# First layer of a two-part transformer: input projections, recurrence and softmax attention in another order

## What is computed

```python
for l in range(DEPTH):                       # 2
    h = rms_norm(x, norm_mix[l]);  z = h @ w_in[l]        # 2560 columns: 20 tiles of 128
    (q_a, k_a, v_a, q_h, i_h, f_fw, f_bw, g_h, a_c, g_c) = jnp.split(z, splits, axis=-1)
    # norm and rotary embedding of q_a (4 tiles) and k_a (1 tile), then softmax attention
    o_att = block_attention(q_a, k_a, v_a)
    # gated recurrence, forwards and backwards, 4 heads of 64
    o_hg = hgrn2_bidirectional(q_h, i_h, f_fw, f_bw, g_h, lb_fwd[l], lb_bwd[l], hgrn_norm[l])
    # depthwise convolution of 31 taps over a_c * sigmoid(g_c), then layer norm and silu
    o_cv = conformer_conv(a_c, g_c, conv_w[l], conv_b[l], conv_ln_g[l], conv_ln_b[l])
    x = x + jnp.concatenate([o_att, o_hg, o_cv], axis=-1) @ w_out[l]
    h = rms_norm(x, norm_mlp[l])
    x = x + jnp.square(jax.nn.relu(h @ w_mlp_in[l])) @ w_mlp_out[l]
```

## Time and profile before

| | us |
|---|---|
| median of 3 runs (4218.06 to 4220.09) | 4219.88 |
| the profiled execution | 4220.85 |
| its span, to which all times below belong | 4218.7 |
| busy in the span: PE, DVE, ACT, POOL | 3820.5, 2100.5, 1303.2, 1276.6 |

### The profile page before, as it was taken

How to read it: one execution, slowest core, us unless ns; L and a number is a source line. 1 busy time by engine, 2 the same in 40 slices (tenths; PEclk the granted TensorE clock), 3 DMA queues, 4 the chain that set the end, 5 groups by cost and what they waited for, 6 DMA issues and landing times. The chain is left out here.

```text
span 4218.7 us, 46489 instructions
## 1 busy us (share of the span) xinstructions
PE 3820.5 (91%) x17918; PEld 2952.7 (70%) x17918; DVE 2100.5 (50%) x3346; ACT 1303.2 (31%) x2109; POOL 1276.6 (30%) x522
## 2 busy tenths in 40 slices
PE   6977999897889997899999989997999999989997
PEld 4656888664768885757777667885757777668886
DVE  3786644448865543352255355553362336346444
ACT  3432211243231112254423432112153432332112
POOL 2210444322024442213232234442213232324442
PEclk8966999999589998999999999998999999999998
DMA  2100233211013232202121123233212121212322
GB/s 97 45 26 2 94 95 95 76 50 50 1 46 97 96 94 103 67 31 75 56 70 60 61 63 93 94 95 108 76 31 75 53 73 50 70 56 92 95 94 69
DMA packets 80149, 292.61 MB, mean 69 GB/s; under 512 B 9617, under 2 KB 10929, under 8 KB 79409
## 3 DMA queue, kind: packets, MB, share of 16 engines
q1 hardware_dynamic: 77136, 278.49, 20.9%
q10 hardware_dynamic: 2784, 11.03, 0.8%
HBM read 285.30 MB, written 2.10 MB: 68 GB/s over the span
## 5 line engine op out<-in xcount | busy, mean ns | idle before, releaser
L205 POOL TENSOR_TENSOR w_lo<-w_raw,w_hi 128x1024 fp32r<-128x1024 f32 x518 | 1276.3, 2464 | 2895.5 <-ACT w_hi L191 2895.4
L191 ACT ACTIVATE w_hi<-w_raw 128x1024 fp32r<-128x1024 f32 x518 | 550.1, 1062 | 1818.4 <-PE acc L242 1759.2
L240 PE MATMUL acc<-hH,w_hi 128*128 128x512 f32 x1840 | 780.5, 424 | 174.2 <-DVE hL L303 91.4
L242 PE MATMUL acc<-hL,w_hi 128*128 128x512 f32 x1840 | 732.1, 398 | 0.0
L241 PE MATMUL acc<-hH,w_lo 128*128 128x512 f32 x1840 | 731.8, 398 | 0.0
L240 PEld LDWEIGHTS acc<-hH,w_hi 128*128 128x128 f32 x1840 | 356.0, 193 | 277.9 <-issue 145.6
L273 DVE TENSOR_TENSOR xT<-acc,xT 128x512 f32<-128x512 f32 x160 | 110.7, 692 | 638.8 <-PE acc L242 638.8
L241 PEld LDWEIGHTS acc<-hH,w_lo 128*128 128x128 f32 x1840 | 356.5, 194 | 79.3 <-issue 13.7
L240 PE MATMUL acc<-H,w_hi 128*128 128x512 f32 x1024 | 404.9, 395 | 5.8 <-issue 4.2
L242 PEld LDWEIGHTS acc<-hL,w_hi 128*128 128x128 f32 x1840 | 354.2, 193 | 78.9
L240 PE MATMUL acc<-midH,w_hi 128*128 128x512 f32 x1024 | 403.9, 394 | 4.2 <-issue 4.2
(11 more groups left out here) (329 smaller groups left out, 4734.8 us busy)
## 6 DMA issues: line engine op xcount, KB each, us to landing
w_raw<-in_stream SPq DMA_DIRECT2D x518, 512.0 KB, 3.5
cw<-in_cmpw ACTq DMA_DIRECT2D x2, 2048.0 KB, 9.0
mixed<-in_cmpw ACTq DMA_DIRECT2D x2, 2048.0 KB, 13.7
x_tok<-in_x SPq DMA_DIRECT2D x1, 2048.0 KB, 8.9
out<-f_tok SPq DMA_DIRECT2D x4, 512.0 KB, 2.6
stack<-Z ACTq DMA_DIRECT2D x8, 128.0 KB, 3.5
stack<-Z ACTq DMA_DIRECT2D x8, 127.8 KB, 3.5
masks_f<-in_masks SPq DMA_DIRECT2D x1, 960.0 KB, 10.8
```

Source lines behind the costliest of these rows:

```text
L191: act.activation(w_hi[:, u % WB, 0:w], w_raw[:, u % 2, 0:w], ACT.Copy).then_inc(hi_split, 1)
L205: pool.tensor_tensor(w_lo[:, u % WB, 0:w], w_raw[:, u % 2, 0:w], w_hi[:, u % WB, 0:w], ALU.subtract)\
L240: pe.matmul(acc[n % 2][:, :], wh, H[:, k, :], start=(k == 0), stop=False)
L242: last = pe.matmul(acc[n % 2][:, :], wh, Lo[:, k, :], start=False, stop=(k == nk - 1))
```

## The change

- **Order.** The units are streamed as: convolution (4), forget gates (4), recurrence q and v (4), then softmax q, k, v (6) and the recurrence's output gate (2). Stage `first_in` has the first 12 products with nothing else on PE; stage `hgrn` comes next with the last 8 (`late_in`) in its steps: run 0 takes 48 parts in 14 steps, run 1 takes 16 parts in 16 steps (`pace`). Norm and rotation of the softmax tiles are in run 0, at fixed steps behind each product. Then `att`, with no products beside it, then `conv`.
- **DVE and ACT in `first_in`.** All four rate chains (behind products 5 to 8) and 26 of the 62 taps (`CONV_EARLY`) stand here; the other 36 are in `att`. `terms` has six buffers, so two chains can overlap. The keys overwrite their gates in `Z`; `att_y` is gone, and the softmax output is split into hi and lo at once.
- **`Recurrence`, in both kinds of layer.** Pairs of DVE instructions become one of twice the length: the gap, the multiplication into `QK`, and the keeping over two banks (the six banks are now one tensor). The exponential becomes two ACT instructions of half the length with scales -1 and +1.
- **The start of all four layers.** Two units are split before `scale_act`; the third split comes after it.

```diff
-GROUPS1 = [("att_in", [(8, 1)] * 6), ("rest_in", [(8, 1)] * 14), ("out", [(8, 1)] * 8)] + FF_GROUPS
+GROUPS1 = [("first_in", [(8, 1)] * 12), ("late_in", [(8, 1)] * 8), ("out", [(8, 1)] * 8)] + FF_GROUPS
+CONV_EARLY = {4: 8, 9: 6, 10: 6, 11: 6}
...
-                        dve.tensor_tensor(G[:, :, 0:h], ref, X[:, :, 0:h], ALU.subtract)
-                        dve.tensor_tensor(G[:, :, h:2 * h], X[:, :, h:2 * h], ref, ALU.subtract).then_inc(gap_ready, 1)
+                        dve.tensor_tensor(G, X, ref, ALU.subtract).then_inc(gap_ready, 1)
...
-                            dve.tensor_tensor(of(QL, h, 1 - d), of(q, h, 1 - d), of(E, h, 1 - d), ALU.mult)
-                            dve.tensor_tensor(of(KL, h, d), of(ks[d], h, d), of(E, h, d), ALU.mult)\
+                            dve.tensor_tensor(self.halves(self.QK[:, (s - 1) % 2, 0, :], self.QK[:, (s - 1) % 2, 1, :], h),
+                                              self.halves(first, second, h), self.halves(E, E, h), ALU.mult)\
                                 .then_inc(terms_ready, 1)
...
-                    act.activation(self.gap[:, s % 2, :], self.gap[:, s % 2, :], ACT.Exp).then_inc(decay_ready, 1)
+                    for which in range(2):
+                        G = self.half(self.gap[:, s % 2, :], h, which)
+                        last = act.activation(G, G, ACT.Exp, scale=1.0 if which else -1.0)
+                    last.then_inc(decay_ready, 1)
...
-                att = PairAttention(attention_sems[0], passes, A["P"], A["PT"], A["stat"], None, 14, take_output=keep_pair)
-                rec = Recurrence(2, [cum[:, r] for r in range(2)], Hg["gap"], Hg["QL"], Hg["KL"], Hg["SS"])
+                att = PairAttention(attention_sems[0], passes, A["P"], A["PT"], A["stat"], None, 0, take_output=split_pair)
+                rec = Recurrence(2, [cum[:, r] for r in range(2)], Hg["gap"], Hg["QK"], Hg["near"], Hg["SS"],
+                                 [(6 * NK, 14), (2 * NK, 16)])
...
-                            rec.pe(r, Z[:, 6 + r, :], keys[:, r, 2, :])
+                            rec.pe(r, Z[:, 8 + r, :], both_keys[:, r, :], late_in, None if r else rope_pe)
...
+                            if 5 <= i < 9:
+                                rates_dve(i - 5)
+                            conv_taps(done, done + CONV_EARLY.get(i, 0))
...
-                        for u in range(WB):
-                            split_hi(units, u)
+                        split_hi(units, 0)
+                        split_hi(units, 1)
                         act.wait_ge(vec_loaded, 16)
                         scale_act(0, V1["norm_mix"], yt, pair)
+                        split_hi(units, 2)
                         finish(act, "start")
```

More of the change, by code:

```diff
@@ L82 @@
            ("gate3", [(8, 1)] * 8), ("mix3", [(4, 2)] * 4), ("out", [(8, 1)] * 8)] + FF_GROUPS
-STAGES1 = ["start", "prep", "att", "hgrn", "conv", "out"] + [g[0] for g in FF_GROUPS]
+STAGES1 = ["start", "first_in", "hgrn", "att", "conv", "out"] + [g[0] for g in FF_GROUPS]
 STAGES2 = ["start", "nsa_in", "prep", "cmp", "att", "mix0", "stick", "mix1", "recur", "mix2", "forget", "mix3",
@@ L754, in dve @@
                         last.then_inc(level_kept, 1)
-                    if other and s >= 1 and self.fills(s - 1):
-                        other.evacuate(take, 1)
+                    if other and s >= 1:
+                        other.evacuate(take, self.ended(run, s - 1))
                     if side:
@@ L773, in pe @@
                     i = self.n * run + s
-                    if other:
-                        other.part(NK // 2)
+                    todo = self.filled(run, s + 1) - self.filled(run, s) if other else 0
+                    while todo:
+                        n = min(todo, NK - other.k)
+                        other.part(n)
+                        todo -= n
+                    if side:
+                        side(s)
                     pe.wait_ge(terms_ready, i + 1)
@@ L1142, in conv_taps @@
+                        early = sum(CONV_EARLY.values())
+                        def conv_taps(begin, end):
+                            for i in range(begin, end):
                                 tap, j = taps[i]
@@ L1194, in _, with late_taps @@
                         after(dve, stages, "hgrn", pe_finished, act_finished)
+                        def late_taps(slot):
+                            left = len(taps) - early
+                            conv_taps(early + slot * left // att.n, early + (slot + 1) * left // att.n)
+                        att.dve(side=late_taps)
+                        finish(dve, "att")
+                        after(dve, stages, "att", pe_finished, act_finished)
                         c, s_ = Cv["c"], Cv["s"]
```

360 lines of the change are left out of this document (177 added, 183 removed).

## The result

The changed kernel took a median of 4147.7 us in 4 runs (4143.32 to 4159.95), beside 4219.99 for the kernel before (4 runs, 4218.06 to 4222.12). The ratio is 0.983, with a 95% interval of 0.9818 to 0.9841: 72 us faster. The direction was forecast and the time lies in the range of 4132 to 4230, but the forecast of 4186 saw a gain of 34 us, less than half of the 72.

What follows compares the result with a forecast made beforehand. The recurrence was taken to pay for PE at 1.2 GHz and DVE, with products beside DVE's uneven work. Stages sum to 363.7 against 369.3 us, 11 for two layers; with 22.7 from starts, 34 less: 4186 us, range 4132 to 4230.

Steps and rivals of the forecast that it cites:

- Starts: Start of all four layers: scaling after the second split instead of the third moves everything up, 22.7 us in all.
- `first_in`: First-kind layers' stage of the first 12 products: DVE, held up by POOL's subtractions, ends it at 94 us.
- Rival 1: The two kinds of work really overlap, with fewer DVE waits and full clock in recurrence and softmax; 4122 us, chance 0.25.
- Barrier and turn: Between the first input stage and the recurrence: barrier, transposes and first terms cost 3.5 us as before.
- Run 0: Recurrence's first run, 14 steps with 48 parts and five without: 58 + 8 + 15 = 81 us, bounds 75 and 95.
- rival 3: Recurrence's first run at 95 us, each of seven DVE waits behind POOL paid in full; 4214 us, chance 0.11.
- The wait between the norms' fixed steps and DVE: Recurrence: such a wait at `z_rstd` or `z_rotated`, given no time, would show the forecast wrong.
- Run 1: Recurrence's second run, one part a step: 47 us at 2.4 GHz, 68 at 1.2 GHz, 56 taken.
- Softmax: Softmax stage without products: 79 us at full PE clock, 107 at half clock, 88 taken.
- The recurrence's merging: Merged DVE instructions save about 0.2 us a step; second kind's PE-bound recurrence given nothing, 4 us either way.
- Rival 2: The clock takes it all: recurrence's second run and softmax stay at 1.2 GHz; 4248 us, slower, chance 0.14.
- the forecast's case: Whole kernel at 4155 to 4211 us, around the forecast of 4186; chance 0.50.

Runs made afterwards that it cites:

- the two profiles: Profiled executions of the changed kernel, the second from a rerun with no edit against it; the rerun measured 4149.64 us, 0.9833 of the kernel before.

## Why the prediction was right and where it was too small

**Starts: right.** 22.7 forecast, 22.8 with that edit alone. The sign given for it ("each start's scaling begins 5 to 6 us after the second split") was misworded: the scaling comes 2.4 us after it, and it is earlier than before by the 5 to 6 us.

**`first_in`: right, and for its reason.** 94 forecast, 93.0 measured. DVE works without gaps from product 4 on, a chain takes 7.26 us with its hit, PE waits 13.5 us at the end where "some 15" had been said, and taking work from DVE (no taps, or half a subtraction) shortens the stage by 15 or 9 us. Rival 1's hits at only half the subtractions did not come: eight subtractions, eight hits.

**Barrier and turn: 3.5 forecast, 7.0 measured.** The step took over the 3.5 of before, where no product stood there. Now three parts do, and after 13.5 us without work PE makes them at a clock of 0.52 (126 to 133).

**Run 0: right, in part by luck.** 81 forecast, 79.0 measured (80.3 by the fixed cuts). Two errors cancel. The 14 steps with parts took 61.8 us where 58 + 8 = 66 stood, and the last five 18.5 where 15 stood; the prediction's own terms for these five, 5 x 2.0 and three times four instructions of 0.7, add up to 18.4. The bound of 95, rival 3, fell: not seven but six subtractions stand in the run, each with its hit, they cost DVE some 10 us instead of 15, and PE hides them all, which the half subtraction showed. The wait between the norms' fixed steps and DVE, named as a sign of a wrong forecast, did not come: DVE waits for PE alone in this run.

**Run 1: the value on the high side.** 56 forecast between 47 and 68; 51.7 and 46.2 in the two profiles. The clock was 0.79 and 0.94, nearer to full than to half. The bracket's ends were not quite what they stood for: at full clock a step with one part takes 2.43 us (PE's scores of 226.92 to those of 229.35) with PE busy throughout, so PE sets it and not DVE, and at a clock of 0.50 it takes 4.38 (255.43 to 259.81) where 3.6 had been given.

**Softmax: the first step that failed.** "I take 88", between 79 at full clock and 107 at half, rested on one row: the clock of 0.50 from 243 to 256, where products had stopped. That row was no steady state: PE stood idle for 7.37 us ahead of the transposes in it, 5.1 of them inside the row, as the trace of the kernel before shows:

```profile
248.14 1.94 PE L514 MATMUL bank<-C,probs 128*128 128x128 f32 x8 [7.37 <-DVE probs L624]
```

It shows the same thing as the first 10 us of softmax here: a clock of 0.50 after a stretch in which PE had little work, there 7.37 us without any, here 2.21 us of it in the 8.6 before (284.6 to 293.2). Then, with PE busy 54 of 64 us in small matmuls, it had 0.97. The other profile had 0.84 over its 80.2 us: it lost more to the clock (0.84 from 300 to 310 and 0.75 from 310 to 320), and was still at the end of 79 and not between. The end of 79 was right but for 3 us in the first profile: its slots of 4.0 us (measured 16.65 for four, with the lump) gave 70 for sixteen, and 16 x 16.65 / 4 = 67. The mis-sized term is 12.2 us a layer in the one profile, 24 of the 27 us that the two layers gave beyond the forecast, and 7.8 in the other, where run 1 gave 9.8.

**The recurrence's merging: the second step that failed, priced at nothing.** "The second kind's recurrence is bound by PE; I give it nothing, with 4 us either way." It fell from 94.1 and 97.2 us to 90.7 and 92.4, and with the pairs restored it is 97.2 and 95.7. In the whole kernel the merging is worth 15 to 17 us. That PE is the bound on average (4.5 us a step) did not mean that DVE's part of a step was hidden in each of them: PE waited for 1.7 us less per recurrence, and its clock, which had been 0.95 and 0.98, was 1.00 and 0.98.

**Sum.** In the profiled execution: forecast 34, plus 24 (softmax), 9 (run 1), 4 (run 0) and 2 (`first_in`), less 7 (barrier), 3 (values) and 1 (tail), makes 62, or 61 unrounded; the second kind's recurrences gained, and dips of the clock elsewhere in the second kind took that back in this one execution (906.0 / 907.2, but 901.5 / 901.1 in the other). In that other execution the gain in the span is 78 us: 20 to 22 from the starts, 45 from the two layers, 11 from the second kind's bodies. Of the 38 us by which the medians beat the forecast, the merging, priced at nothing, is 15 to 17, as its own run shows. The remaining 21 to 23 are, roughly, softmax and run 1, the two terms that were put between the clock's two levels (33 and 35 us over both layers in the two profiles), less the 11 that barrier, values and tail took more.

**Rivals.** Rival 1 (4122) had softmax and run 1 at full clock, and both came near; its other two parts, fewer hits in `first_in` and a run 0 of 75, did not. Its 4122 is 26 us under the measured time all the same, and without the merging, of which it does not speak, it would be 42. Rival 2 (the clock takes it all) had the first 10 us of softmax and some short stretches for it. The truth lay between the forecast's case and rival 1. For each of the two terms the full-clock end of its range would have been the better choice here; that is seen afterwards, since nothing in the rows of before told which end it would be.

## What to carry to other kernels

A low clock in a row where dense work has just stopped need not be the price of the stage that follows: look how long it lasts and whether the engine had work in it (0.50 in the first 10.2 us of softmax here, 0.97 in the other 64.2). Dense parts among small matmuls at a low clock can be cheap: 11 us of them cost run 1 only 1.5 to 7 us, though a third product there cost it 3 to 9 more. When two stages are both set by one engine, moving its work from one to the other gains nothing (26 taps: no change), while moving it into that engine's waits does (18 taps into two waits of about 8 us: 17 to 19 us).

## What had not been expected of the hardware

- One kernel's executions differ by up to 17 us (4142.8 to 4159.95) with the same instructions, and the difference lies in where the granted clock is low: run 1 at 0.94 or 0.79, the second kind's bodies 901 or 907 us. The kernel before varied by less in its first three runs (4218.06 to 4220.09), and by 10 us in the next 9 (4216.3 to 4225.9).
- A run with a product less took nearly the same time, at a lower clock and with more idle time (0.90 to 0.84, 80.3 to 79.7 us).
- Merging pairs of DVE instructions (two of 256 columns take 2 x 0.42 us, one of 512 takes 0.68) was worth 1.7 us of a recurrence at the same clock (92.4 to 90.7), and with it the clock stayed at 1.00 or 0.98 in 18 recurrences of 18, where it was 0.95 to 0.98 in five of six without.
- A DVE hit behind a POOL subtraction that has just begun costs 2.1 to 2.2 us, with 256 columns as with 512 (2.63 for 0.42; `L1146`, 2.79 for 0.69). The prediction spoke of instructions that read two operands in SBUF; a cast of one is hit as well (`L383` in the MLP of before: 2.51 at 1294.08, behind the subtraction of 1293.82, for 0.43), and an evacuation out of a bank was not (`L1117` at 53.17, inside the subtraction of 52.37: 0.69). The hit cost the kernel its whole length in `first_in`, which DVE sets (9 us a layer for half the subtraction's length), and nothing in run 0, whose steps with parts PE sets.
